# A decoder step in one core: prompt attention in pairs of heads, laid beside the sample attention

## The chip, the core and the metric

The kernel runs on one core of a Trainium2 chip. The engines are TensorE (PE, matrix products; PEld is its weight load), VectorE (DVE), ScalarE (ACT), GpSimd (POOL) and SyncE (SP), which here issues nearly all DMAs. SBUF is the working memory of 128 partitions, PSUM the memory of 8 banks into which PE writes. The metric is the device time of one execution in microseconds, as the median of several runs; one of them is profiled.

## The reference

Two layers of a hybrid decoder run on 256 prompt tokens and on 8 sample sequences of 8 new tokens each (320 tokens, width 2048, all in float32). The part that matters here is the attention of mixers A and C:

```
h = rms_norm(x, g_mix);  p = h @ w_in           # q, k, v of A and C, columns of B
A: 8 heads of 64, branches (window, dilation) = (128,1), (512,4), (2048,16)
C: 16 query heads, 2 kv heads, window 128, a learned sink per head
prompt: s = q k^T * scale; masked; p = exp(s - lse); o = p v     # 256 x 256 in blocks of 128
sample: the same with keys = concat(cache, new)                  # 8 sequences, 2048 (A) and 128 (C) old rows
x = x + concat(A, B, C) @ w_out;  x = x + SwiGLU(rms_norm(x))
```

Of the 2048 cached rows of A a sample needs 1280, the others lie outside every branch. Mixer B is a recurrence that is done before the attention begins.

## The kernel before

A layer streams the weights of `w_in` (each block is split into a high and a low part by ACT and DVE, and three products are summed), does mixer B, then the function `attention` of every engine, then `w_out` and the feed-forward blocks. All engines run programs of their own, in order, and wait for each other by named semaphores (`sc`, `sm`, `pn` and so on); the order is written out by hand.

The attention has two stages, one behind the other.

The prompt stage takes 24 heads (8 of A, 16 of C) in turn. GpSimd copies a head's queries into a zeroed tile `qp`, PE makes the scores (banks 0 and 1 in turn), DVE masks them into `psm` and takes two row maxima (`nm`), ACT takes exponentials with their sums, DVE scales by the reciprocals, PE turns the probabilities (three 128x128 transposes), ACT copies them to `ppt`, PE multiplies by the values and ACT copies the output into `pT`. Three heads are under way at once.

The sample stage takes four quarters q; a quarter is the pair of sequences 2q and 2q+1. The cached rows lie with positions on the partitions, and the scores need them with the head dimension there: in `keys`, PE transposes them in 26 turns of up to four 128x128 tiles, ACT copies each turn from PSUM into one of eight tiles `ktr`, and after every four turns PE makes the scores of that group, four products side by side on 128x32 column tiles of its array. The keys of quarter q+1 are turned ahead of the probabilities of quarter q. `probabilities` turns the sample's probabilities, `values` multiplies them by the cached values, `select` picks the wanted blocks; DVE's `scores`, `weighted` and `outputs` go with them. The caches are loaded by SP: `cK` and `cV` hold one quarter each, ten pieces of 512 KB for the keys of a quarter and ten for its values; the keys of the next quarter are loaded as the `ktp` count says that PE has turned a piece, its values as `pvq` says so.

SP stores the states of mixer B (18 DMAs from `Sout` and `SoutP`) and waits for them before it loads the first keys:

```
sp.wait_ge(sem["rw"], 2 * (l + 1))
sp.wait_ge(sem["souts"], 16 * 18 * (l + 1))
for which in "KV":
    for quad in range(3):
        cache(0, which, quad)
        cache(1, which, quad)
```

After the last quarter ACT and DVE split the first block of `w_out`, ACT writes the mixed rows `hh`, and PE begins the output projection.

## Time and profile before

| | |
|---|---|
| median of 3 runs | 3400.95 us (3396.55 to 3401.13) |
| the profiled execution | 3401.5 us, its span 3399.6 us |
| busy, share of the span | PE 96%, PEld 90%, DVE 50%, ACT 36%, POOL 3% |
| granted PE clock, mean | 0.979 of 2.4 GHz |
| DMA | 501.17 MB, mean 147 GB/s |
| attention, layer 0 | 468.6 to 660.4 us |
| attention, layer 1 | 2139.8 to 2334.1 us |

The busy shares are means over stages with different limits: most of the span is the weight stages, in which PE streams without a pause. The attention of a layer runs from PE's first scores of the prompt to its first product with `w_out`; it is read by itself, by stretches of the timeline.

### The profile page before, as it was taken

The page shows a single profiled execution, that of the slowest core. Times are in us where ns is not written, and L with a number is a line of the kernel's source. Part 1 is how long each engine was busy: PE and PEld are TensorE (multiplying, and loading weights), DVE is VectorE, ACT ScalarE, POOL GpSimd, SP SyncE. Part 2 cuts the span into 40 slices and gives each one's busy share as a digit, 9 for nine tenths or more (in the row PEclk, how much of TensorE's full clock was granted, in tenths as well). Part 3 has the DMA queues.
Part 4 walks back from the last instruction along what each step waited for, and adds up shares of the span by engine and source line. Part 5 has one row for each costly group of instructions (what it writes and reads, how often), then busy time and mean ns, then how long its engine had stood idle before and what let it go on. Part 6 is the DMA issues. An engine that isn't in the chain of part 4 may idle for free.

```text
span 3399.6 us, 60962 instructions
## 1 busy us (share of the span) xinstructions
PE 3272.0 (96%) x25078; PEld 3074.4 (90%) x25078; DVE 1711.3 (50%) x2269; ACT 1208.5 (36%) x1607; POOL 91.9 (3%) x209
## 2 busy tenths in 40 slices
PE   7999888999999999999999988889999999999998
PEld 6999755699999999999999986557999999999998
DVE  5455572355555454454545664714555544545544
ACT  3332256433322222222434313654422323323234
POOL 1000011000000000000000000100000000000000
PEclk9999889999999999999999998999999999999999
DMA  6552036765555554554564610577655545545454
GB/s 196 164 135 65 2 132 234 258 151 150 150 150 140 159 148 138 160 148 140 152 190 136 137 27 2 191 278 201 148 149 151 149 140 164 149 136 161 137 146 132
DMA packets 848704, 501.17 MB, mean 147 GB/s; under 512 B 96608, under 2 KB 823152, under 8 KB 848112
## 3 DMA queue, kind: packets, MB, share of 16 engines
q1 hardware_dynamic: 848108, 499.01, 51.7%
q8 instruction: 106, 1.74, 0.2%
q14 instruction: 38, 0.31, 0.0%
q10 hardware_dynamic: 452, 0.11, 0.0%
HBM read 485.71 MB, written 13.37 MB: 147 GB/s over the span
## 4 chain that ended last, share of the span: by engine, by line
PE 91%; DVE 4%; ACT 2%; issue 1%; DMA 1%; ACTq 0%; SPq 0%; DVEq 0%
PE PS L1435 87%; PE PS L1436 4%; ACT ktr L884 1%; ACT psm L855 0%; DVE psm L1303 0%; DVE wl L962 0%; ACT ppt L866 0%; DVE nm L1305 0%; ACT wh L641 0%; DVE S0T L1255 0%; DMA sink<-in_c_sink 0%; DVE rt L1080 0%; DMA raw<-in_w_out 0%; DVE WT L1183 0%; DMA raw<-in_w_in 0%
## 5 line engine op out<-in xcount | busy, mean ns | idle before, releaser
L641 ACT ACTIVATE wh<-raw 128x2048 fp32r<-128x2048 f32 (+1 forms) x408 | 711.7, 1744 | 1235.7 <-PE PS L1435 1214.2
L962 DVE TENSOR_TENSOR wl<-raw,wh 128x2048 fp32r<-128x2048 f32 (+1 forms) x408 | 848.9, 2081 | 400.2 <-ACT wh L641 399.6
L1435 PE MATMUL PS<-fh,wh 128*128 128x320 f32 x2816 | 870.6, 309 | 0.0
L1435 PE MATMUL PS<-fh,wl 128*128 128x320 f32 x2816 | 870.1, 309 | 0.0
L1435 PE MATMUL PS<-fl,wh 128*128 128x320 f32 x2816 | 870.1, 309 | 0.0
L1435 PEld LDWEIGHTS PS<-fh,wh 128*128 128x128 f32 x2816 | 528.5, 188 | 0.2
L1435 PEld LDWEIGHTS PS<-fl,wh 128*128 128x128 f32 x2816 | 528.5, 188 | 0.2
L1435 PEld LDWEIGHTS PS<-fh,wl 128*128 128x128 f32 x2816 | 528.5, 188 | 0.0
L1435 PE MATMUL PS<-hh,wh 128*128 128x320 f32 (+2 forms) x1696 | 521.3, 314 | 4.8 <-DVE wl L962 4.8
L1435 PE MATMUL PS<-hh,wl 128*128 128x320 f32 (+2 forms) x1696 | 513.5, 309 | 0.0
L1435 PE MATMUL PS<-hl,wh 128*128 128x320 f32 x1664 | 510.5, 310 | 0.0
L1435 PE MATMUL PS<-ah,wh 128*128 128x320 f32 x1408 | 435.7, 309 | 0.2 <-DVE wl L962 0.2
L1435 PE MATMUL PS<-al,wh 128*128 128x320 f32 x1408 | 435.1, 309 | 0.0
L1435 PE MATMUL PS<-ah,wl 128*128 128x320 f32 x1408 | 435.1, 309 | 0.0
L1435 PEld LDWEIGHTS PS<-hh,wh 128*128 128x128 f32 x1696 | 317.9, 191 | 8.6 <-DVE wl L962 5.2
L1435 PEld LDWEIGHTS PS<-hh,wl 128*128 128x128 f32 x1696 | 315.2, 189 | 0.0
L1435 PEld LDWEIGHTS PS<-hl,wh 128*128 128x128 f32 x1664 | 312.2, 188 | 1.4
L1435 PEld LDWEIGHTS PS<-ah,wh 128*128 128x128 f32 x1408 | 264.3, 188 | 0.8 <-issue 0.5
L1435 PEld LDWEIGHTS PS<-al,wh 128*128 128x128 f32 x1408 | 264.3, 188 | 0.0
L1435 PEld LDWEIGHTS PS<-ah,wl 128*128 128x128 f32 x1408 | 264.3, 188 | 0.0
L670 ACT ACTIVATE ge<-gt 128x320 f32<-128x320 f32 x88 | 41.5, 472 | 488.2 <-DVE gt L1002 488.2
L1002 DVE TENSOR_TENSOR gt<-PS,rsb 128x320 f32<-128x320 f32 x88 | 43.3, 492 | 224.7 <-PE PS L1435 224.6
(329 smaller groups left out, 2711.4 us busy)
## 6 DMA issues: line engine op xcount, KB each, us to landing
raw<-in_w_gate SPq DMA_DIRECT2D x88, 1024.0 KB, 5.6
raw<-in_w_up SPq DMA_DIRECT2D x88, 1024.0 KB, 5.6
raw<-in_w_down SPq DMA_DIRECT2D x128, 704.0 KB, 4.8
raw<-in_w_in SPq DMA_DIRECT2D x56, 1024.0 KB, 5.6
cK<-in_cache_a_k SPq DMA_DIRECT2D x80, 512.0 KB, 6.5
cV<-in_cache_a_v SPq DMA_DIRECT2D x60, 512.0 KB, 8.8
raw<-in_w_in SPq DMA_DIRECT2D x32, 512.0 KB, 5.3
raw<-in_w_out SPq DMA_DIRECT2D x32, 512.0 KB, 4.5
```

Source lines behind the costliest of these rows:

```text
L641: act.activation(wh[j][:, 0:kts], raw[j][:, 0:kts], ACT.Copy).then_inc(sem["wh"], 1)
L670: act.activation(ge[:], gt[:], ACT.Tanh, scale=0.5).then_inc(sem["gexp"], 1)
L884: act.activation(ktr[g % 8][:, 0:n], PS[:, 4 + g % 2, 0:n], ACT.Copy).then_inc(sem["ktc"], 1)
L962: tt(wl[j][:, 0:kts], raw[j][:, 0:kts], wh[j][:, 0:kts].bitcast(F32), ALU.subtract).then_inc(sem["wl"], 1)
L1002: tt(gt[:], PS[:, 0, 0:TOK], rsb[:], ALU.mult).then_inc(sem["ev"], 1)
L1435: mm = lambda out, lhsT, rhs, start=True, stop=True: pe.matmul(out, lhsT, rhs, start=start, stop=stop, skip_group_check=True)
L1436: tr = lambda out, x: pe.transpose(out, x, con[0:x.shape[0], at["ident"][0]:at["ident"][0] + x.shape[0]])
```

## The change

The prompt heads are taken in 12 pairs (4 of A, 8 of C), two heads in one instruction on DVE and two row halves of PE's array, with no copy of the queries. Pairs 0 to 2 start ahead; the other pairs lie in the quarters of the sample attention: in quarter q the carried pair 3q+2 is finished inside `keys`, pair a = 3q+3 goes between the scores and the probabilities, pair b = 3q+4 behind them, and pair c = 3q+5 is begun in `values` and carried over. ACT, not DVE, scales the probabilities.

The old keys are no longer turned by PE. DVE turns them where they lie, in 32x32 blocks (`turn`, six instructions a quarter, as the pieces land), and PE makes the scores on sixteen 32x32 tiles of its array: eight blocks of sixteen products over 320 columns each, every row group into a bank of its own (4 to 7). The queries for that are turned by `query_rows`, the window keys by `window_keys`. There is one tile `smA` and one `smC` instead of two. SP starts the first keys without waiting for the state stores, stores the states behind the keys of quarter 1, and loads the keys of quarter q+1 when all key scores of quarter q are done (`sc`). The diff, cut:

```diff
-        ktr = [place(f"ktr{i}", [P, 512], RW + 40960 + 2048 * i if i < 3 else RK + 2048 * (i - 3)) for i in range(8)]
+        kcT = place("kcT", [P, 2, P], RW + 40960)
+        qd = [place(f"qd{i}", [P, 2, 2, 2, 160], RK + 5120 * i) for i in range(2)]
...
                 def next_keys(q):
-                    for quad in range(3):
-                        sp.wait_ge(sem["ktp"], TURNS * (4 * l + q - 1) + (8 * (quad + 1) if quad < 2 else TURNS))
-                        cache(2 * q, "K", quad)
-                        cache(2 * q + 1, "K", quad)
+                    sp.wait_ge(sem["sc"], 4 * l + q)
+                    for b2 in range(2):
+                        for quad in range(3):
+                            cache(2 * q + b2, "K", quad)
...
+                for q in range(1, NB // 2):
+                    next_keys(q)
+                    if q == 1:
+                        states_out()
+                        sp.wait_ge(sem["souts"], 16 * 18 * (l + 1))
+                        for quad in range(3):
+                            cache(NB - 1, "V", quad)
+                    next_values(q)
...
+                def scale(p):
+                    i = p % 2
+                    take("prs")
+                    for h in range(2):
+                        for q, cols in enumerate(BLOCKS):
+                            a = act.activation(psm[i][:, h, cols], psm[i][:, h, cols], ACT.Copy, scale=sums[i][:, h, q:q + 1])
+                    a.then_inc(sem["pn"], 1)
...
+                for q in range(NB // 2):
+                    a, b, c = partners(q)
+                    carry = 3 * q + 2
+                    exp(carry)
+                    scale(carry)
+                    turned_probs(carry)
+                    if q < LASTQ:
+                        exp(a)
+                    output(carry)
+                    if q < LASTQ:
+                        scale(a)
+                        turned_probs(a)
+                        output(a)
+                    if q == 0:
+                        act.wait_ge(sem["snk"], 64 * (l + 1))
+                    exps(q)
+                    turned_sample(q)
+                    if q < LASTQ:
+                        query_rows(q + 1)
+                        exp(b)
+                        scale(b)
+                        turned_probs(b)
+                        output(b)
+                        window_keys()
...
+                def front(p):
+                    x = psm[p % 2]
+                    take("S")
+                    if p >= 2:
+                        dve.wait_ge(sem["PT"], 2 * (PAIRS * l + p - 1))
+                    m = C("maskA" if p < 4 else "maskC").unsqueeze(1).broadcast_to([P, 2, 384])
+                    done(stt(x[:], PS[:, 0:2, 0:384], SCALE, m, ALU.mult, ALU.add), "sm")
+                    dve.tensor_reduce(nm[p % 2][:, :, 0], x[:, :, 0:P], AX_X, ALU.max, negate=True)
+                    done(dve.tensor_reduce(nm[p % 2][:, :, 1], x[:, :, P:384], AX_X, ALU.max, negate=True), "nmx")
+                def back(p):
+                    i = p % 2
+                    take("pex")
+                    if p >= 4:
+                        done(tt(sums[i][:], sums[i][:], psk[i][:], ALU.add))
+                    done(dve.reciprocal(sums[i][:], sums[i][:]), "prs")
+                def turn(q, first, last):
+                    for n in range(first, last):
+                        b2, quad = n // 3, n % 3
+                        k0, kts = QUADS[quad]
+                        dve.wait_ge(*keys_in(l, q, quad, b2))
+                        x = cK[b2][:, k0:k0 + kts].rearrange("p k c -> p (k c)")
+                        dve.transpose(x, x).then_inc(sem["kt"], 1)
...
+                front(0)
+                turn(0, 0, 1)
+                back(0)
+                front(1)
+                turn(0, 1, 2)
+                back(1)
+                turn(0, 2, 4)
+                front(2)
+                turn(0, 4, 6)
                 for q in range(NB // 2):
+                    a, b, c = partners(q)
                     if q:
                         outputs(q - 1)
-                    if q < NB // 2 - 1:
-                        scores(q + 1)
+                    back(3 * q + 2)
+                    if q < LASTQ:
+                        front(a)
+                        back(a)
+                    scores(q)
+                    if q < LASTQ:
+                        front(b)
+                        turn(q + 1, 0, 5)
+                        back(b)
+                        turn(q + 1, 5, 6)
                     else:
                         split(start_of(l, "out"), 0, KT)
                     weighted(q)
-
-                dve.wait_ge(sem["oc"], 24 * (l + 1))
+                    if q < LASTQ:
+                        front(c)
...
+                def prompt_scores(p):
+                    if p:
+                        pe.wait_ge(sem["sm"], PAIRS * l + p)
+                    kt = KA + p if p < 4 else KC
+                    for cols, keys in ((slice(0, P), P), (slice(P, SEQ), SEQ)):
+                        for h in range(2):
+                            r = slice(h * HD, h * HD + HD)
+                            a = mm(PS[:, h, cols.start:cols.start + keys], pT[r, tile_of(p), cols], pT[r, kt, 0:keys])
+                    a.then_inc(sem["S"], 1)
+                def turned_probs(p, h):
+                    take("pn", 1 - h)
+                    if p or h:
+                        pe.wait_ge(sem["ptc"], 2 * (PAIRS * l + p) + h)
+                    for i in range(3):
+                        a = tr(PS[:, 2, i * P:(i + 1) * P], psm[p % 2][:, h, i * P:(i + 1) * P])
+                    a.then_inc(sem["PT"], 1)
+                def prompt_values(p):
+                    pe.wait_ge(sem["ptc"], 2 * (PAIRS * l + p) + 2)
+                    if p:
+                        pe.wait_ge(sem["oc"], PAIRS * l + p)
+                    if p >= 5 and p % 3 == 2:
+                        pe.wait_ge(sem["bo"], 4 * l + p // 3)
+                    for kt in range(2):
+                        for h in range(2):
+                            c0 = (2 * p + h) * HD if p < 4 else P + h * HD
+                            vals = tk[1 if p < 4 else 2][:, kt, c0:c0 + HD]
+                            out = PS[h * HD:h * HD + HD, 3, P * kt:SEQ]
+                            a = mm(out, vals, ppt[:, h, 0:SEQ] if kt == 0 else ppt[:, h, SEQ:384], kt == 0, kt == 1)
+                    a.then_inc(sem["O"], 1)
...
+                    a, b, c = partners(q)
+                    carry = 3 * q + 2
+                    pe.wait_ge(sem["ktc"], 8 * l + 2 * q + 2)
+                    pe.wait_ge(sem["kt"], 6 * (4 * l + q) + 6)
+                    if q:
+                        pe.wait_ge(sem["om"], 4 * l + q)
+                    for h in range(4):
+                        for jj in range(2):
+                            for i in range(4):
+                                r = slice(32 * i, 32 * i + 32)
+                                for b2 in range(2):
+                                    for fh in range(2):
+                                        out = PS[64 * b2 + 32 * fh:64 * b2 + 32 * fh + 32, 4 + i, 0:320].rearrange("p (k c) -> p k c", k=10)
+                                        c0 = (4 * fh + h) * HD + 32 * jj
+                                        m = mm(out, qd[q % 2][r, b2, jj, fh, 32 * h:32 * h + 32], cK[b2][r, :, c0:c0 + 32], not (h or jj), h == 3 and jj == 1)
+                            if (h, jj) == (3, 1):
+                                m.then_inc(sem["sc"], 1)
+                            if (h, jj) == (0, 0):
+                                if q:
+                                    select(q - 1)
+                                if q < LASTQ:
+                                    prompt_scores(a)
+                            elif (h, jj) == (1, 0):
+                                turned_probs(carry, 0)
+                            elif (h, jj) == (2, 0):
+                                turned_probs(carry, 1)
+                            elif (h, jj) == (3, 0):
+                                prompt_values(carry)
...
+                    keys(q)
+                    if q < LASTQ:
+                        for h in range(2):
+                            turned_probs(a, h)
+                        prompt_values(a)
+                        prompt_scores(b)
+                    probabilities(q)
                     values(q)
+                    if q < LASTQ:
+                        for h in range(2):
+                            turned_probs(b, h)
+                        prompt_values(b)
+                        window_keys(q + 1)
```

How the instructions stand before and after. On DVE, in the prompt stage before, where `psm_170` and `psm_171` are the tiles of two heads and a head's scaling stands behind the next one's maxima:

```order
L1303 SCALAR_TENSOR_TENSOR psm_170<-PS,con 128x384 [waits s_S,s_nmx]
L1304 TENSOR_REDUCE nm_179<-psm_170 128x1 [waits s_sm]
L1305 TENSOR_REDUCE nm_179<-psm_170 128x1
L1311 RECIPROCAL sums_181<-sums_181 128x2 [waits s_pex,s_nmx]
L1313 TENSOR_SCALAR psm_169<-psm_169,sums_181 128x128 [waits s_dve]
L1314 TENSOR_SCALAR psm_169<-psm_169,sums_181 128x256
```

And on DVE in quarter 0 after the change, from pair b's masking to the weighting of the quarter (`cK_139` and `cK_140` hold the keys of the next quarter's two sequences, `sums_167` the sums of pair b):

```order
L1336 SCALAR_TENSOR_TENSOR psm_160<-PS,con 128x768 [waits s_PT,s_S,s_bnm]
L1337 TENSOR_REDUCE nm_165<-psm_160 128x2 [waits s_sm]
L1338 TENSOR_REDUCE nm_165<-psm_160 128x2
L1354 STREAM_TRANSPOSE cK_139<-cK_139 128x2048 [waits s_cK00,s_nmx]
L1354 STREAM_TRANSPOSE cK_139<-cK_139 128x2048 [waits s_cK10]
L1354 STREAM_TRANSPOSE cK_139<-cK_139 128x1024 [waits s_cK20]
L1354 STREAM_TRANSPOSE cK_140<-cK_140 128x2048 [waits s_cK01]
L1354 STREAM_TRANSPOSE cK_140<-cK_140 128x2048 [waits s_cK11]
L1344 TENSOR_TENSOR sums_167<-sums_167,psk_169 128x4 [waits s_pex]
L1345 RECIPROCAL sums_167<-sums_167 128x4 [waits s_dve]
L1354 STREAM_TRANSPOSE cK_140<-cK_140 128x1024 [waits s_cK21,s_prs]
L1376 TENSOR_TENSOR ssu_173<-ssu_173,ssk_175 128x2 [waits s_bex]
```

The two scalings have left DVE, and five turns stand between a pair's maxima and its reciprocals, each behind a landing.

On PE, in the sample stage before, at a group of keys (`ktr_141` and the following are turned keys):

```order
L1436 MATMUL PS<-con,cK_140 128x128 [waits s_ktc]
L1436 MATMUL PS<-con,cK_140 128x128 x3
L1435 MATMUL PS<-ktr_141,qdA_151 32x512 [waits s_ktc]
L1435 MATMUL PS<-ktr_142,qdA_151 32x512
L1435 MATMUL PS<-ktr_143,qdA_151 32x512
```

And on PE after the change, inside the key scores of quarter 0, at the end of one block and the start of the next:

```order
L1492 MATMUL PS<-cK_139,qd_142 32x320 x2
L1492 MATMUL PS<-cK_140,qd_142 32x320 x2
L1493 MATMUL PS<-con,psm_160 128x128 [waits s_ptc,s_pn]
L1493 MATMUL PS<-con,psm_160 128x128 x2
L1492 MATMUL PS<-cK_139,qd_142 32x320 x2
```

The transposes of keys are gone, the scores read `cK` itself, and the carried pair's transposes, with their wait for ACT's scaling (`pn`), stand between the blocks.

On SP before, ahead of the first keys:

```order
L462 DMA out_new_wkv_sample<-Sout 64x4x64 [waits s_Sov,s_Soc]
L462 DMA out_new_wkv_sample<-Sout 64x4x64 x7
L464 DMA out_new_wkv_prompt<-SoutP 64x4x64
L462 DMA out_new_wkv_sample<-Sout 64x4x64 x8
L464 DMA out_new_wkv_prompt<-SoutP 64x4x64
L482 DMA cK_139<-in_cache_a_k 128x1x1024 [waits s_souts,s_rw]
```

And on SP after, from the last of quarter 1's keys to the first of its values:

```order
L480 DMA ckc_151<-in_cache_c_k 128x128
L508 DMA out_new_wkv_sample<-Sout 64x4x64 x8
L510 DMA out_new_wkv_prompt<-SoutP 64x4x64
L508 DMA out_new_wkv_sample<-Sout 64x4x64 x8
L510 DMA out_new_wkv_prompt<-SoutP 64x4x64
L476 DMA cX<-in_cache_a_v 128x1x1024 [waits s_souts]
L476 DMA cX<-in_cache_a_v 128x1x1024 x2
L478 DMA cX<-in_cache_a_v 128x1024 x2
L476 DMA cV_137<-in_cache_a_v 128x1x1024 [waits s_pvq]
```

The state stores have moved behind the keys of quarter 1, and the last sequence's values (`cX`), which wait for them, stand ahead of quarter 1's values and of quarter 2's keys.

## Rows read from the trace of the kernel before

**Rows 1.** Stretches of layer 0's two stages (busy us of each engine, clock, DMA share, GB/s).
```profile
468.60:528.80 60.20, 52.98 (x264) 32.13 (x264) 47.88 (x160) 45.84 (x161) 13.36 (x48) 0.97 0.74 268
528.80:660.40 131.60, 115.18 (x1060) 72.26 (x1061) 26.38 (x65) 72.07 (x162) 5.44 (x25) 0.96 0.72 252
...
sum 386.10, PE 337.29 PEld 209.31 DVE 148.62 ACT 235.80 POOL 37.22; mean PE 84.32 PEld 52.33 DVE 37.16 ACT 58.95 POOL 9.30
```

**Rows 2.** Timeline of PE at a score group (start us, us, what, idle before).
```profile
534.09 1.07 PE L1435 MATMUL PS<-ktr,qdA 128*32 128x512 f32 x8
535.08 1.09 PE L1436 MATMUL PS<-con,cK 128*128 128x128 f32 x8
```

**Rows 3.** Instructions on the tile psm (ns: least/median/most, first and last start).
```profile
L855 ACT ACTIVATE psm<-psm,nm x96: 401/447/495, 470.8 to 2197.7; 128x128 f32<-128x128 f32 x48, 128x256 f32<-128x256 f32 x48
L855 ACT ACTIVATION_READ_ACCUMULATOR psm<-psm,nm x96: 185/187/190, 471.1 to 2198.1; 128x1 f32 x96
L1303 DVE SCALAR_TENSOR_TENSOR psm<-PS,con x48: 557/558/558, 469.6 to 2196.0; 128x384 f32<-128x384 f32 x48
...
L1305 DVE TENSOR_REDUCE nm<-psm x48: 408/409/410, 470.3 to 2196.8; 128x1 f32<-128x256 f32 x48
```

**Rows 4.** Instructions on the tile ppt.
```profile
L866 ACT ACTIVATE ppt<-PS x48: 465/476/492, 474.9 to 2200.4; 128x384 f32<-128x384 f32 x48
```

**Rows 5.** DVE's groups by line and shape (busy us, mean ns, idle before).
```profile
L962 DVE TENSOR_TENSOR wl<-raw,wh 128x2048 fp32r<-128x2048 f32 x280 | 641.1, 2290 | 316.4 <-ACT wh L641 316.1
...
L1326 DVE SCALAR_TENSOR_TENSOR smA<-PS,con 128x512 f32<-128x512 f32 x16 | 10.3, 686 | 110.2 <-PE PS L1435 88.4 <-issue 21.7
...
L1057 DVE RECIPROCAL rsb<-rsb 128x320 f32<-128x320 f32 x4 | 8.6, 2154 | 2.4 <-ACT rsb L714 2.4
L1311 DVE RECIPROCAL sums<-sums 128x2 f32<-128x2 f32 x48 | 8.0, 166 | 1.7
...
L1117 DVE TENSOR_SCALAR pT<-pT 128x1280 f32<-128x1280 f32 x2 | 1.6, 820 | 0.0
```

**Rows 6.** Timeline of PE in mixer B, small tiles of the array.
```profile
309.55 0.69 PE L1435 MATMUL PS<-dA,dB 64*64 64x64 f32 x32
310.07 0.65 PE L1435 MATMUL PS<-dB,dA 64*64 64x64 f32 x32
...
452.34 1.24 PE L1435 MATMUL PS<-rstd,con 32*128 32x256 f32 x8
```

**Rows 7.** Timeline of DVE, ACT and PE in the sample stage.
```profile
549.66 1.62 DVE L1326 SCALAR_TENSOR_TENSOR smA<-PS,con 128x512 f32<-128x512 f32 x3 [23.57 <-PE PS L1435]
...
553.44 0.54 DVE L1332 TENSOR_REDUCE snm<-smC 128x2 f32<-128x384 f32 x1
...
641.14 1.42 ACT L891 ACTIVATE smA<-smA,snm 128x1344 f32<-128x1344 f32 x1 [1.51 <-DVE snm L1332]
...
643.43 0.28 ACT L895 ACTIVATE ssk<-snm,snk 128x2 f32<-128x2 f32 x1
...
645.99 1.42 PE L1436 MATMUL PS<-con,smA 128*128 128x128 f32 x11
...
648.77 0.64 PE L1435 MATMUL PS<-tk,ptA 64*32 64x256 f32 x8
...
658.72 1.06 PE L1435 MATMUL PS<-con,om 128*128 128x32 f32 x4 [3.44 <-DVE omC L1344]
```

**Rows 8.** Stretches around a pause of PE (columns as in rows 1).
```profile
553.00:556.10 3.10, 0.19 (x3) 0.04 (x1) 0.99 (x2) 2.08 (x4) 0.00 (x0) 0.82 0.01 3
556.10:560.00 3.90, 3.90 (x17) 1.91 (x18) 0.00 (x0) 2.64 (x8) 0.00 (x0) 0.50 0.15 23
```

**Rows 9.** SP's first key loads, and how long the key loads took to land.
```profile
L482 SPq DMA_DIRECT2D cK<-in_cache_a_k x6: 535/603/622, 482.7 to 486.6; - x6
...
DMA to landing us min/median/max: 4.0/7.7/10.3
```

**Rows 10.** A stretch of key loads in the sample stage.
```profile
592.00:596.00 4.00, 3.75 (x29) 2.37 (x30) 0.00 (x0) 2.58 (x5) 0.00 (x0) 1.00 1.01 401
```

425 lines of the change are left out of this document (169 added, 256 removed).

## The prediction, made before the changed kernel ran

> **What bounds the kernel now.** I read the windows first. The page gives TensorE (PE) 96% of the span, but that share is made by the weight stages; the change touches two stages only, one per layer. In layer 0 the prompt attention takes 60.2 us and the sample attention 131.6, up to the first product of the output projection; with layer 1 the four stretches add up to 386.1 us [rows 1], 193 a layer. Nothing is full there: over the sample stretch VectorE (DVE) works 26.4 of 131.6 us, ScalarE (ACT) 72.1, DMA 0.72 of its time. So each stage is a chain, and time comes out of it only by shortening the chain or laying two side by side. In the prompt stretch DVE (47.9 of 60.2) sets the pace: per head a 0.56 us masking, two maxima (0.41 the wider), two scalings [rows 3]. In the sample stretch PE and ACT alternate: four transposes, one copy to SBUF, 26 times a quarter; then a score group, whose successor starts 0.99 us later [rows 2].
>
> **The change, part by part.** Time 0 is PE's start of attention (468.6 us in layer 0); the end is the first output-projection product. Before: 191.8 and 194.3 us.
>
> *Removed:* 104 transposed key tiles a layer and their ACT copies, GpSimd's query copies (hidden already), the 60 us of prompt heads as a stage of their own. *Added:* DVE turns, 10,240 columns a quarter; 128 small score products a quarter.
>
> *A turn.* No row shows one. From below it is bounded by the fastest DVE form, 820 ns for 1280 columns (0.64 per column); from above by the dearest, 2154 for 320 (6.7) [rows 5]. I take 1.07 ns, since the forms that move a 4-byte column per beat lie there: 686 ns for 512, 2290 for 2048. So 2.2 us for 2048 columns, 1.1 for 1024, 11 a quarter. The Trainium skill (Vector Engine (DVE) Microarchitecture Reference, the reshape front-end section) lets the transpose sustain one element per cycle per lane; no run here shows it yet, and by it the sum stays.
>
> *A score block* (16 products of 32x32, 320 columns). Sixteen-fold tiling has no row. Four column tiles do run together: 512 columns take 0.99 us for the whole group [rows 2], which scales to 0.62 for 320. Four row tiles do too, and 64x64 tiles, two by two: 32 records start within 0.52 us [rows 6], which also shows 32 records can issue in that time. I take 0.6; the bounds are 0.5 (issue alone) and 2.5 (row groups one after another). The Trainium skill (TensorEngine Tiling (Array Packing), Key Properties) says that changing the tiling mode drains the engine, which speaks against mixing these blocks with full-array work. In the rows the full-array transposes start 0.99 us after a column-tiled group whose records last 1.07 [rows 2], so a drain is not visible; at 0.15 us, 14 switches a round would add 2 us a round, 16 in all.
>
> *A prompt pair.* DVE: one masking of 768 columns (0.56 for 384 plus 1.0 ns a column: 0.94), maxima over 256 and 512 columns, 0.41 and 0.67: 2.0 us [rows 3, 5]. ACT: exponentials 2 x 1.0 (two of 0.45 with 0.19 readings between), two sinks of 0.28 [rows 7]; DVE's reciprocal and sum 0.17 each [rows 5]; ACT scaling, four copies of 0.27 to 0.38 by the 0.48 for 384 columns [rows 4]: 1.3; two turns by PE (0.5) and copies (0.48); value products 0.85.
>
> *A round* (quarter q in the middle), from PE's start of the key scores, with the carried pair masked by then: exponentials to 2.5, reciprocals 2.9, scaled 4.2; PE turns head 0 to 4.8, two blocks, head 1 to 6.5, two blocks to 7.7, values 8.5, last block **9.1**. Only there is `sc` given, and the next keys may load. The new-token and window scores end at 10.9. DVE's masks and maxima, 4.3 us for three pieces [rows 7] and 0.4 for the fourth, end at 15.7 (the next pair fits in before). ACT's exponentials take 2.6 (641.14 to 643.71), PE's turns and ACT's copies 2.8 (645.99 to 648.77) [rows 7]: 21.1. The value products took 6.5 (648.77 to 658.72, less the 3.44 of idle); with the query rows and a pair's scores 28.5. DVE meanwhile: pair b to 17.7, five turns (9.8) to 27.5, back(b) 27.9, the last turn 29.1, weighting 30.5, next pair 32.5. The keys are there in time: issued at 9.1, first landing after 4.0 us [rows 9], 5.4 MB at 401 GB/s [rows 10] take 13.4. Pair b ends the round, as its reciprocal stands behind five turns: 27.9, scaling 29.2, two turns and copies 31.6, values 32.6, window keys copied **33.6**.
>
> *The other rounds.* In round 0 the carried pair already has its exponentials, so `sc` comes at 6.8 and the round is 2.3 shorter: 31.3. In round 1 SyncE (SP) issues the state stores (18 at some 0.6 us [rows 9]), waits for their landing, then cX and V, before it reaches the keys of quarter 2; those then land some 6 us late, of which 3.2 show: 36.8. Round 2: 33.6. *Front:* DVE masks the first pair, waits for the first two key pieces (issue, 4.0 us to landing, one piece more: 5.5), then does six turns (11), two pairs (4.0), two reciprocals (0.4) and waits about 1.7 for the second pair's exponentials: 22.6. *End:* round 3 to 21.1, then as before 11.65 (648.77 to 660.40). Sum 22.6 + 31.3 + 36.8 + 33.6 + 32.7 = 157.0.
>
> *The clock.* Between pair b's scores (14.4) and the turned probabilities (18.3) PE idles 3.9 us a round. Where it idled 3 us before, the next 3.9 ran at a granted 0.50, the 1.2 GHz level [rows 8]. That stretches the probabilities and the first values by about 2.4 us: four times, **166.6**. Against 193.05 that is 26.4 a layer, 52.9 in all.
>
> The profiled execution took 3401.5 us (span 3399.6), the median is 3400.95, so 3401.5 - 52.9 = 3348.6; I say **3348 us**. A change under 0.2% (7 us) can't be told from none.
>
> *What stands behind the new waits.* DVE's turns wait for landings, with the pair's reciprocals and the weighting of the quarter behind them, and PE's next key scores behind those. SP's key loads wait for `sc`, with the state stores and the V loads behind. PE's turning of a pair waits for ACT's scaling, with the rest of the key blocks behind it; ACT's query rows and pair b wait behind the sample's exponentials.
>
> *Edits costed at nothing:* the query rows on PE and ACT lie under the value products and DVE's turns; the moved state stores leave the front free (14 us of SP there) and cost what round 1 says; GpSimd's memsets end before time 0.
>
> **Rivals.**
> - *The DVE becomes the bound (slower).* The place is the five turns in front of back(b). At twice my price rounds 0 to 2 grow by 9.8 each (9216 columns), the front by 11 (10,240): some 40 a layer, about 3430. It decides from the point where these 37,900 columns eat the 26.4 us that a layer gains: 0.7 ns more, 1.8 a column. For it: no row shows a turn, and 2154 ns for 320 columns is a DVE row too. Against: every form that only moves or adds lies at 1.1 or below.
> - *The blocks run row group by row group (slower):* 2.5 us instead of 0.6; then the blocks, not the carried pair, set `sc`: 22.5 for 9.1. Four times 13.4: about 3455. Against: [rows 6]. The Trainium skill (TensorE: Matmul & The Clock Gate, Measured speedup vs the span model) gives 10.6-fold for sixteen tiles; an estimate from that is 0.94 a block, which would make the sum about 3370.
> - *The clock stays low through the stage.* Some 10 us more a round, as blocks, values and turns double: about 3428. For it: one 3 us pause gives half the clock [rows 8], and a round has a pause of 3.9 us, one of 1.4 in front of the carried pair's turn, and about 1 us around each copy that PE waits for. Against: the window of [rows 10], in an alternation of quarter-microsecond waits, stayed at 1.00.
> - *The gap goes unpunished and the steps pack tighter:* 157 a layer and a quicker turn at 0.64: 3305 to 3330.
> - *The change doesn't do what it says:* PE takes its instructions in order, so each wait for a pair stands in front of the samples too; at 45.5 us a round, (191.8 - 22.6 - 32.7)/3, nothing is saved: within 0.2%.
>
> **How the numbers follow.** Forecast (3325 to 3375) 0.54, tighter 0.20, no gain 0.06, DVE bound 0.09, blocks in series 0.04, low clock 0.07. The tighter case reaches to about 3300 and holds most of its chance above that; of the dear ones the low clock and the small excesses are taken in: 3300 to 3410 leaves out about 2 in 10. Faster 0.78 (forecast, tighter, and half of the low clock's chance, where it holds for a part of the rounds), same 0.05, slower 0.17.
>
> **What the profile after would show.** Right: STREAM_TRANSPOSE at 2.2 us for 2048 columns; a block's 16 products within 0.6 us; rounds of 33 to 38 us, whose ends are chained PE - ACT - DVE through pair b; key loads starting some 9 us into a round; stretches at 0.5 clock around the probabilities; nothing moved in the weight stages. Wrong if turns cost over 1.8 ns a column, if `sc` comes after 15 us, if the DVE waits for landings (then SP's order is the bound), or if a round ends in the value products instead of pair b.

## The result, and the profile after

The changed kernel takes 3379.4 us (median of 5 runs, 3377.8 to 3385.9) against 3396.6 us for the kernel before on the same chip: a ratio of 0.995, 95% interval 0.9935 to 0.9964. It is faster, by 17 us, and the time lies within the range; but the forecast was a gain of 52.9 us, three times as much. The profiled execution has a span of 3380.0 us, 19.6 less than before. The attention of layer 0 now takes 180.8 us (before 191.8 [rows 1], forecast 166.6), that of layer 1 182.4 (before 194.3). Between the two layers' attentions the profile shows 1483.2 us for 1479.4 before; in the later runs this stretch took 1477 to 1485 without a pattern, and I draw nothing from it.

The page's first part, whose PE share answers to the 96% of before:

```profile
PE 3198.1 (95%) x26358; PEld 3021.7 (89%) x26358; DVE 1757.8 (52%) x2117; ACT 1150.6 (34%) x1543; POOL 74.3 (2%) x157
```

The windows of layer 0's attention, cut where the key scores of a round begin (front, rounds 0 to 2, last stretch; columns as in [rows 1]):

```profile
467.52:490.91 23.39, 10.70 (x61) 5.83 (x56) 17.54 (x18) 13.42 (x48) 0.00 (x0) 0.58 0.98 367
490.91:528.20 37.29, 29.61 (x483) 17.36 (x484) 23.42 (x33) 18.46 (x62) 1.93 (x12) 0.90 0.80 275
528.20:575.24 47.04, 33.43 (x492) 19.72 (x492) 24.56 (x39) 20.92 (x74) 1.93 (x12) 0.80 0.97 377
575.24:614.02 38.78, 31.76 (x491) 19.40 (x492) 24.20 (x39) 20.90 (x74) 0.00 (x0) 0.84 0.46 170
614.02:648.31 34.29, 24.19 (x413) 14.72 (x414) 8.79 (x21) 15.56 (x35) 1.93 (x1) 0.80 0.60 148
```

Two things stand out. Round 1 is 8 to 10 us longer than its neighbours, and DMA is full in it (0.97, 377 GB/s). And the granted clock, 0.97 and 0.96 in the two stages before [rows 1], is 0.58 to 0.90 now, although TensorE is busy for 29 to 33 us of each of rounds 0 to 2.

The turns, among the groups by line and shape in layer 0:

```profile
L1354 DVE STREAM_TRANSPOSE cK<-cK 128x2048 f32<-128x2048 f32 x16 | 36.5, 2296 | 11.5 <-DMA cK<-in_cache_a_k 11.3
...
L1354 DVE STREAM_TRANSPOSE cK<-cK 128x1024 f32<-128x1024 f32 x8 | 9.8, 1224 | 0.1
```

The timeline of the changed kernel, the places that the rest speaks of:

```profile
490.91 1.38 PE L1492 MATMUL PS<-cK,qd 32*32 32x320 f32 x32 [2.21 <-DVE cK L1354]
...
511.49 10.12 DVE L1354 STREAM_TRANSPOSE cK<-cK 128x2048 f32<-128x2048 f32 x5
...
512.14 2.57 PE L1493 MATMUL PS<-con,smA 128*128 128x128 f32 x11 [3.38 <-ACT ssk L900]
...
521.91 1.49 ACT L879 ACTIVATE psm<-psm,sums 128x128 f32<-128x128 f32 x4 [1.99 <-DVE sums L1345]
...
524.17 0.55 PE L1493 MATMUL PS<-con,psm 128*128 128x128 f32 x3
...
529.17 1.89 SPq L476 DMA_DIRECT2D cX<-in_cache_a_v  x3
...
540.33 2.83 SPq L476 DMA_DIRECT2D cK<-in_cache_a_k  x3
...
556.12 2.31 DVE L1354 STREAM_TRANSPOSE cK<-cK 128x2048 f32<-128x2048 f32 x1 [7.52 <-DMA cK<-in_cache_a_k]
...
569.57 0.90 PE L1493 MATMUL PS<-con,psm 128*128 128x128 f32 x3 [5.47 <-ACT psm L879]
...
580.03 2.80 PE L1492 MATMUL PS<-cK,qd 32*32 32x320 f32 x64
...
619.01 1.71 PE L1492 MATMUL PS<-cK,qd 32*32 32x320 f32 x64
...
642.47 2.29 DVE L994 TENSOR_TENSOR wl<-raw,wh 128x2048 fp32r<-128x2048 f32 x1 [11.66 <-ACT wh L634]
...
646.34 0.48 DVE L1380 SCALAR_TENSOR_TENSOR om<-PS,ssu,con 128x256 f32<-128x256 f32 x1 [1.30 <-PE PS L1492]
```

Read from the top. The first key block of round 0 (16 products, two records each) takes 1.38 us, at half clock. In round 0 the five turns (four of 2048 columns and one of 1024) run through without a wait (10.1 us, forecast 9.8). The pause ahead of the probabilities is 3.4 us (forecast 3.9), and the 11 transposes behind it take 2.6 us, where they took 1.42 before [rows 7]. At 524.17 TensorE turns pair b without having waited, since ScalarE finished scaling it 0.8 us before: pair b does not end this round, but it is close. In round 1 the keys of quarter 2 are issued from 540.33 and their first turn starts at 556.12, after a wait; that ends in 5.47 us for which TensorE waits for pair b. Two key blocks (64 records) take 2.80 us at half and 1.71 at full clock. The last two rows are the split of `w_out` and, behind it on VectorE, the weighting of the last quarter, which waits another 1.30 us for TensorE's values; both become important below.

### The profile page after: what moved, and what is told of

It is laid out like the page before. It is cut to its first block and busy times, and to the rows that moved or that the text cites. A ratio compares the mean times of both kernels' runs of the same rounds, so it can differ in the third digit from the quotient of the medians.

```text
span 3380.0 us, 62858 instructions
## 1 busy us (share of the span) xinstructions
PE 3198.1 (95%) x26358; PEld 3021.7 (89%) x26358; DVE 1757.8 (52%) x2117; ACT 1150.6 (34%) x1543; POOL 74.3 (2%) x157
```

## The experiments

**Theory**, from these rows: (a) the transfers of round 1 are late because cX (2.6 MB) and the values of quarter 1 are being carried ahead of the keys of quarter 2; (b) TensorE loses time at half clock, in more places than the pause that the prediction priced. **Rivals**: pair b's chain behind five turns (the forecast), products that stand in each other's way on one row group, or a round that is simply full on TensorE.

All ratios are to the kernel before, timed beside each run on the same chip; the changed kernel itself stands at 0.995.

| run | ratio, 95% interval | median us |
|---|---|---|
| e1_cx_late | 0.9917 (0.9902 to 0.9933) | 3372.7 |
| e2_fill | 0.9947 (0.9933 to 0.9960) | 3381.6 |
| e3_back_early | 0.9942 (0.9928 to 0.9956) | 3379.5 |
| e4_row_order | 0.9946 (0.9932 to 0.9960) | 3379.4 |
| e5_fill_sized | 0.9953 (0.9940 to 0.9966) | 3381.2 |
| e6_late_fill_back | 0.9873 (0.9859 to 0.9887) | 3355.0 |
| e7_fill_all | 0.9854 (0.9841 to 0.9868) | 3349.0 |
| e8_half_rows | a single run | 3402.6 |
| e9_late_back | 0.9908 (0.9893 to 0.9924) | 3366.0 |
| e10_out_first | 0.9842 (0.9829 to 0.9856) | 3344.5 |
| e11_fill_no_late | 0.9905 (0.9889 to 0.9920) | 3363.5 |
| e12_half_columns | 1.0164 (1.0147 to 1.0181) | 3454.9 |
| e13_light_fill | 0.9913 (0.9893 to 0.9932) | 3366.3 |

### e1_cx_late: cX behind the keys of quarter 2

```diff
                     if q == 1:
                         states_out()
+                    if q == 2:
                         sp.wait_ge(sem["souts"], 16 * 18 * (l + 1))
                         for quad in range(3):
                             cache(NB - 1, "V", quad)
```

> Only SyncE's order is changed: the values of the last sequence (2.6 MB into cX, needed by the last quarter alone) are loaded behind the keys of quarter 2 and not ahead of the values of quarter 1. Theory, the transfers of round 1 (cX, the values of quarter 1 and the keys of quarter 2, 13.4 MB at some 400 GB/s) are what makes it 47.0 us: the keys of quarter 2 land some 6 us earlier, pair b's wait of 5.5 us and the half clock behind it go, round 1 of layer 0 comes down to 39 to 41 us, round 2, which then starts at full clock, from 38.8 to about 37; 8 to 11 us a layer, 16 to 22 in all: 3358 to 3364 us. Rival, the round is long because of its own chain through TensorE and the DMAs only show it: under 4 us in all.

Its timeline in round 1 of layer 0:

```profile
552.52 10.02 DVE L1355 STREAM_TRANSPOSE cK<-cK 128x2048 f32<-128x2048 f32 x5
...
564.37 0.55 PE L1494 MATMUL PS<-con,psm 128*128 128x128 f32 x3 [0.53 <-ACT psm L880]
```

The five turns no longer wait, pair b's wait falls from 5.47 to 0.53 us, and round 1 comes to 41.1 us in both layers (47.0 and 48.7 before). So the wait was the transfers'. But the kernel gains 6.7 us by the medians (11 by the ratios of the table), where 16 to 22 were expected: round 2 did not fall (39.8 and 40.7), and round 0 of layer 1 took 41.0 instead of 37.2, both at half clock for part of the time.

### e2_fill, e5_fill_sized: filling the pause ahead of the probabilities

```diff
                         prompt_scores(b)
+                    fill(20 if q < LASTQ else 48)   # 12 and 27 in the second run
                     probabilities(q)
+                def fill(n):
+                    for _ in range(n):
+                        mm(PS[:, 2, 0:P], C("ident"), C("ident"))
```

> TensorE multiplies 20 (last quarter 48) 128x128 products of the identity into the free bank 2 in the pause ahead of the sample's probabilities; nothing reads them. Theory, each such pause costs by the half clock behind it alone: the probabilities take 1.4 us everywhere instead of up to 2.6, the values no longer 12 but 10.7 us, 2 to 2.5 us a round, 16 to 20 us in all. Rival, in rounds 0 and 2 pair b's chain on VectorE and ScalarE (five turns, reciprocal, scaling) comes only 0.5 to 0.8 us behind today's values, in round 1 the keys end last: 0.5 to 0.8 us in rounds 0 and 2, nothing in round 1, 2 in the last: 6 to 8 us in all. A third: the clock does not follow such products, no change.

```profile
509.10 4.73 PE L1492 MATMUL PS<-con 128*128 128x128 f32 x40
513.67 1.36 PE L1493 MATMUL PS<-con,smA 128*128 128x128 f32 x11
...
528.32 1.38 PE L1492 MATMUL PS<-cK,qd 32*32 32x320 f32 x32 [0.47 <-ACT kcT L857]
```

The clock does follow: the transposes behind the products take 1.36 us instead of 2.57. But 20 products last 4.7 us, more than the pause, and the next round begins at half clock all the same (1.38 us for its first block). The second run has the number corrected.

> As the first filling, but 12 products in the pause ahead of the probabilities (27 in the last quarter), since one took 0.23 us and 20 of them overran the pause of 3.4 us by 1.3. Theory, half clock behind the pauses is a cost of the changed kernel: with the pause filled and not overrun, rounds 0 and 2 are 0.8 to 1.5 us shorter, the last stretch 34.3 to about 31: 4 to 6 us a layer, 8 to 12 in all: 3367 to 3372 us. Rival, what is won is lost again at the next pause (the clock falls there instead): within 3 us of the changed kernel.

No gain either (3381 us): the rival holds, as far as these pauses go. But what is won is not lost to the clock alone. In rounds 0 and 2 TensorE now waits for pair b's scaling, which was ready before it in the changed kernel:

```profile
523.20 0.55 PE L1493 MATMUL PS<-con,psm 128*128 128x128 f32 x3 [1.24 <-ACT psm L879]
...
607.89 0.55 PE L1493 MATMUL PS<-con,psm 128*128 128x128 f32 x3 [0.53 <-ACT psm L879]
```

So with the pauses filled the forecast's chain, five turns and then the reciprocal, does end these rounds. The last stretch is the telling one. Its rows, of TensorE, ScalarE and VectorE in the order of time:

```profile
624.05 6.25 PE L1492 MATMUL PS<-con 128*128 128x128 f32 x54
631.36 1.42 PE L1493 MATMUL PS<-con,smA 128*128 128x128 f32 x11 [1.06 <-ACT ssk L900]
...
639.02 1.91 ACT L634 ACTIVATE wh<-raw 128x2048 fp32r<-128x2048 f32 x1 [4.93 <-DMA raw<-in_w_out]
641.04 2.29 DVE L994 TENSOR_TENSOR wl<-raw,wh 128x2048 fp32r<-128x2048 f32 x1 [12.34 <-ACT wh L634]
...
643.65 0.48 DVE L1380 SCALAR_TENSOR_TENSOR om<-PS,ssu,con 128x256 f32<-128x256 f32 x1
...
644.70 1.06 PE L1492 MATMUL PS<-con,om 128*128 128x32 f32 x4 [4.04 <-DVE omC L1382]
```

TensorE ran the values at full clock and was done at 640.7, and the stretch still took 34.5 us (34.3 in the changed kernel). VectorE weights the quarter only after the split of the first `w_out` block, ScalarE starts that split at 639.02, and it waits for the block's landing. In the changed kernel the weighting began 1.30 us behind the split, when the values came; so the half clock stood 1.3 us above the load there, and with the half clock gone the load alone keeps the stretch as long.

### e3_back_early: pair b's reciprocal behind four turns

```diff
-                        turn(q + 1, 0, 5)
+                        turn(q + 1, 0, 4)
                         back(b)
-                        turn(q + 1, 5, 6)
+                        turn(q + 1, 4, 6)
```

> Pair b's reciprocal stands behind four turns instead of five on VectorE. As the prediction had it (pair b ends each round, behind five turns) this takes 2.0 us off rounds 0 to 2: 12 us in all. Rival, by the trace of the changed kernel: TensorE reaches pair b's transposes without waiting in rounds 0 and 2 of layer 0 (0.5 us of wait in round 0 of layer 1) and waits for late keys in round 1: 0 to 4 us in all.

No change, 3379.5 us. The forecast's own statement of what ends a round falls with it, for the changed kernel: pair b is ready 0.8 and 0.6 us before TensorE comes to it in rounds 0 and 2 of layer 0, so by itself the reciprocal's place is worth nothing. It counts once TensorE comes sooner, as in the filled kernel above.

### e4_row_order: the row groups in turn

```diff
-                            for i in range(4):
-                                r = slice(32 * i, 32 * i + 32)
-                                for b2 in range(2):
-                                    for fh in range(2):
+                            for b2 in range(2):
+                                for fh in range(2):
+                                    for i in range(4):
+                                        r = slice(32 * i, 32 * i + 32)
```

> In each block of key scores the four row groups now alternate from one product to the next, instead of four products in a row on one row group; the same products otherwise. Theory, products on one row group follow each other and that is why a block takes 0.84 us and not the 0.6 of the prediction: a block comes to 0.55 to 0.65, 1.5 to 2.3 us a round, 12 to 18 us in all. Rival, the block is bound by something that the order does not touch: 0.80 to 0.87 a block and no change (within 4 us).

Two blocks still take 1.71 us at full clock, and the kernel 3379.4 us. The order of the products is not what sets a block.

### e6_late_fill_back, e9_late_back: the edits together

The edits of e1, e3 and e5 in one kernel.

> Three edits together: cX behind the keys of quarter 2, 12 and 27 products in the pauses, pair b's reciprocal behind four turns. If the transfers and the clock are separate costs, they add: 7 to 10 us from the first, 8 to 12 from the second, and the third now counts, since TensorE comes to pair b earlier: 1 to 3: 3355 to 3364 us. Rival, the cost of the clock moves to the next pause: 3368 to 3373, as with the first edit alone.

3355.0 us, at the fast edge of what was expected: 24.4 us less than the changed kernel, where the three alone brought 6.7, nothing and nothing. To see what the filling did in it, it was taken out again:

> The third run of the last four without its filling: cX behind the keys of quarter 2 and pair b's reciprocal behind four turns, no products in the pauses. It tells what the filling was worth there. Theory, the half clock: without the filling 10 to 16 us of the 24 go, 3365 to 3372 us, and TensorE is at half clock for 60 us or more of a layer's attention. Rival, the reciprocal's place was what pays once the keys come in time, and the filling does little, as it did alone: 3352 to 3360 us.

3366.0 us, within what the theory named. So cX and the reciprocal bring 13 us, the filling another 11. (The profiled execution of this kernel is the longest of its runs, 3380.6 us, 14 us above the next; rounds 0 to 2 take 41 us each there, at a granted clock of 0.76 to 0.83, so these rows may overstate the half clock.)

### e7_fill_all, e11_fill_no_late: all pauses filled

```diff
+                fill(10)              # behind the first two pairs' scores
                 for h in range(2):
                     turned_probs(0, h)
...
                 def turned_probs(p, h):
+                    if h and p and p % 3 != 2:
+                        pe.wait_ge(sem["oc"], PAIRS * l + p)
+                        fill(2, 3)        # pairs a and b, into bank 3
                     take("pn", 1 - h)
...
                 def prompt_values(p):
-                    pe.wait_ge(sem["ptc"], 2 * (PAIRS * l + p) + 2)
                     if p:
                         pe.wait_ge(sem["oc"], PAIRS * l + p)
+                    if p and p % 3 != 2:
+                        fill(2, 3)
+                    pe.wait_ge(sem["ptc"], 2 * (PAIRS * l + p) + 2)
...
                 def keys(q):
...
+                    fill(1 if q else 6)
...
                 def values(q):
+                    fill(3)
...
+                fill(4)
                 select(NB // 2 - 1)
```

with cX late, the reciprocal early and 12 (27) products ahead of the probabilities as above.

> As the run before, and the smaller pauses of TensorE are filled too: two products of 0.23 us in each pause of 0.6 to 0.7 us between a pair's transposes and its values, three ahead of the sample values, one ahead of the key scores, four ahead of the last selection, ten in the first pair's pause and six ahead of the first key scores. Theory, the half clock is brought on by TensorE's pauses all together, the half-microsecond ones too: the stage runs at 0.95 or more, the first key block of a round takes 0.83 us instead of 1.38, rounds come to 34 to 35.5, the last stretch to 31: 3335 to 3350 us. Rival, only the pauses of 3 us and more count: as the run before, within 4 us. A third, the products collide with what they wait for and the rounds grow.

3349.0 us, within the theory's numbers; the rounds of layer 0 take 34.7, 37.5 and 35.9 us at 0.95, 0.95 and 1.00, and only the last stretch stays, at 35.8. That is 6.0 us less than without the filling of the small pauses, though the two intervals still overlap a little. The profiles agree: over both layers the fronts, where longer pauses were filled as well, are 1.3 us shorter, and rounds and last stretches together 6.0. So the half-microsecond pauses seem to count, by some 6 us. Then the late cX was taken back, with all pauses filled:

> All pauses filled and pair b's reciprocal behind four turns, but cX again ahead of the values of quarter 1. Theory, the transfers of round 1 and the clock are two costs: round 1 stays at 44 to 47 us and the other rounds at 34.5 to 37, so 16 to 20 us over the kernel with both: 3365 to 3369 us. Rival, the late keys cost mainly by the half clock that their wait brings: 3352 to 3360 us.

3363.5 us, below the theory's range and nearer to it than to the rival's. Round 1 is 47.1 us again, at a clock of 0.89:

```profile
527.17:574.27 47.10, 34.60 (x539) 23.81 (x539) 24.42 (x39) 20.52 (x73) 1.93 (x12) 0.89 0.93 356
574.27:608.48 34.21, 32.34 (x542) 22.18 (x543) 24.22 (x40) 20.75 (x74) 0.00 (x0) 1.00 0.60 225
```

With the reciprocal early in all four, the kernel takes 3379.5 with neither, 3366.0 with cX late, 3363.5 with the pauses filled, 3349.0 with both: 13.5 and 16.0 us one by one, 30.5 together. By the ratios of the table it is 11.5 and 12.6 one by one and 30 together, each with some 7 us of uncertainty either way. They are two costs, and within that they add.

### e10_out_first: the first blocks of w_out ahead of the last values

```diff
                 for q in range(1, NB // 2):
                     next_keys(q)
...
+                    if q == LASTQ:
+                        sp.wait_ge(sem["out"], 16 * 9 * (l + 1))
+                        sp.wait_ge(sem["pvq"], 12 * l + 9)
+                        stream(l, "out", part="first")
                     next_values(q)
-                sp.wait_ge(sem["out"], 16 * 9 * (l + 1))
-                sp.wait_ge(sem["pvq"], 12 * l + 9)
-                stream(l, "out")
+                stream(l, "out", part="rest")
```

> As the kernel with all pauses filled, and SyncE loads the first two blocks of w_out ahead of the last quarter's values (their place is free once the values of quarter 2 are multiplied), not behind. Theory, the last stretch is bound by that load: its block lands at 639 us, ScalarE and VectorE split it, and the weighting of the last quarter stands behind the split on VectorE (TensorE pauses 4.0 us there with all other pauses filled, and the stretch stayed at 34.3 to 34.5 us when it ran at full clock). The stretch falls from 35.6 to 31 to 33 us: 5 to 9 us in all, 3340 to 3344 us. Rival, the prompt rows (four ScalarE copies of some 1 us each) and the values end the stretch: within 2 us of 3349.

3344.5 us, the best version, 0.9842 of the kernel before. Its windows in layer 0:

```profile
466.41:489.25 22.84, 15.24 (x100) 11.20 (x95) 17.59 (x18) 13.45 (x49) 0.00 (x0) 0.78 0.98 367
489.25:523.79 34.54, 31.89 (x532) 21.28 (x532) 23.15 (x32) 18.07 (x62) 1.93 (x12) 1.00 0.86 301
523.79:559.19 35.40, 33.11 (x539) 22.29 (x539) 23.00 (x37) 20.51 (x73) 1.93 (x12) 1.00 1.00 377
559.19:595.19 36.00, 32.95 (x539) 22.24 (x539) 25.44 (x42) 20.68 (x73) 0.00 (x0) 1.00 0.87 327
595.19:626.51 31.32, 28.73 (x481) 20.60 (x482) 9.11 (x22) 15.29 (x36) 1.93 (x1) 1.00 0.55 140
```

and the rows that answer to those of the last stretch above:

```profile
617.71 1.92 ACT L640 ACTIVATE wh<-raw 128x2048 fp32r<-128x2048 f32 x1
...
619.73 2.29 DVE L1000 TENSOR_TENSOR wl<-raw,wh 128x2048 fp32r<-128x2048 f32 x1 [7.29 <-ACT wh L640]
...
624.54 0.48 DVE L1386 SCALAR_TENSOR_TENSOR om<-PS,ssu,con 128x256 f32<-128x256 f32 x1 [2.24 <-PE PS L1498]
```

ScalarE splits without waiting, and the weighting now waits for TensorE's values, not the other way round. The stretch falls to 31.3 us (33.0 in layer 1). The gain by the medians, 4.5 us, is just below the 5 to 9 expected, and the two intervals overlap; the rows, not the medians, show the cause: the two last stretches are 7.0 us shorter together.

### e8_half_rows, e12_half_columns: what a block costs

```diff
-                            for i in range(4):
+                            for i in range(2):
```

> Only row groups 0 and 1 of the key scores are computed, eight products a block instead of sixteen (half of the old keys' scores are left out). Theory, the products of a block are issued one after another at a fixed price, 52 ns each at full clock: the block falls from 0.83 to about 0.42 us, sc comes 3.3 us earlier. Rival, the row groups run side by side and the 320 columns set the time: 0.7 to 0.83 us, sc hardly earlier.

```profile
492.00:506.00 14.00, 13.72 (x150) 5.17 (x150) 2.34 (x6) 4.90 (x17) 0.00 (x0) 0.50 0.72 278
```

```profile
495.12 2.38 PE L1492 MATMUL PS<-cK,qd 32*32 32x320 f32 x32
```

Half the products, and the kernel takes 3402.6 us in a single run, 23 more than with all of them. Two blocks take 2.38 us, against 2.80 for full blocks at the same half clock. So a block of eight products is not half as dear: something other than their number bounds it there. I take that to be the passing of its columns, which the run does not show. And the clock stood at 0.50 for 14 us in which TensorE was busy for 13.72: work was removed and time was lost (mean granted clock 0.946, in the changed kernel 0.962). The run leaves the price at full clock open, so the products were made smaller instead, on the best version:

```diff
-                                        m = mm(out, qd[q % 2][r, b2, jj, fh, 32 * h:32 * h + 32], cK[b2][r, :, c0:c0 + 32], not (h or jj), h == 3 and jj == 1)
+                                        for ks in (slice(0, 5), slice(5, 10)):
+                                            m = mm(out[:, ks], qd[q % 2][r, b2, jj, fh, 32 * h:32 * h + 32], cK[b2][r, ks, c0:c0 + 32], not (h or jj), h == 3 and jj == 1)
```

> On the kernel with all pauses filled and the first blocks of w_out loaded early: each product of the key scores is made as two of 160 columns (32 products a block instead of 16, the same result). It tells what the 0.84 us of a block at full clock are. Theory, a fixed price for each product (its weight load and its issue, 52 ns): the block doubles to some 1.67 us, sc comes 6.7 us later in each of the four rounds and the kernel is up to 53 us slower (3375 to 3400 us). Rival, the columns that pass set the time (320 columns take 0.62 us by the column tiles of the kernel before, the rest is filling and draining): 0.84 to 1.1 us a block, within 10 us of 3344.

```profile
493.34 1.66 PE L1498 MATMUL PS<-cK,qd 32*32 32x160 f32 x64 [2.50 <-DVE cK L1360]
...
499.59 1.72 PE L1498 MATMUL PS<-cK,qd 32*32 32x160 f32 x37 [1.46 <-issue]
...
502.07 5.62 PE L1498 MATMUL PS<-cK,qd 32*32 32x160 f32 x128
```

```profile
486.00:499.40 13.40, 9.27 (x199) 7.40 (x200) 9.15 (x10) 4.96 (x16) 0.00 (x0) 1.00 1.04 409
499.60:517.50 17.90, 17.90 (x371) 12.99 (x370) 0.18 (x1) 4.49 (x15) 0.00 (x0) 0.50 0.18 63
```

The block doubles at full clock: 64 records in 1.66 us, 26 ns each, as in a block of 320 columns (32 records in 0.83). A product of this kind has a fixed price of 52 ns, for 160 columns and for 320; what makes it is not shown. By that alone the kernel would lose 53 us; it loses 110. The rest goes with the clock. It stood at 1.00 up to 499.4 us, the end of a pause of 1.46 us inside the blocks (the profile shows nothing that TensorE waited for), and from 499.6 on at 0.50 for 17.9 us in which TensorE does not pause at all. Whether the pause or the small products brought the clock down is not shown; that 17.9 us of unbroken work on them did not bring it back is.

### e13_light_fill: the same pauses, filled with little

That left a question: is it the pauses that bring on the half clock, or what the array does? The filling products of the best version were made on one 32x32 tile instead of 128x128.

```diff
-                        mm(PS[:, bank, 256:384], C("ident"), C("ident"))
+                        mm(PS[0:32, bank, 256:384], C("ident")[0:32, 0:32], C("ident")[0:32])
```

> The kernel with all pauses filled and the first blocks of w_out loaded early, but each filling product is made on one 32x32 tile of the array instead of all 128x128 (the same 128 columns, so about the same 0.2 us). Theory, the clock follows TensorE's pauses: with the pauses filled by anything it stays as it was with full products, 10 to 15 us at half clock in a layer's attention, 3344 us within 4. Rival, the clock follows what the array does: half clock comes back as without filling, 50 us or more a layer, rounds of 36 to 41 us, 3360 to 3368 us.

3366.3 us (3357 to 3376): 22 us of the gain are gone, though TensorE is as busy as with full products. Its front and its last stretch in layer 0, and round 0 of layer 1:

```profile
467.68:491.30 23.62, 16.67 (x102) 10.59 (x96) 17.59 (x18) 13.45 (x49) 0.00 (x0) 0.69 0.98 362
...
601.50:636.10 34.60, 33.37 (x482) 23.09 (x482) 8.79 (x21) 15.42 (x35) 1.95 (x1) 0.85 0.50 128
...
2139.80:2180.93 41.13, 39.66 (x535) 23.40 (x533) 23.44 (x33) 18.41 (x63) 1.94 (x12) 0.80 0.79 272
```

In the last stretch TensorE is busy for 33.4 of 34.6 us and is granted 0.85; with full products it had 1.00 at 28.7 of 31.3 us. The rival holds in the time. In the clock it holds in part: rounds 0 to 2 of layer 0 stand at 0.92 to 0.95, but round 0 of layer 1 takes 41.1 us at 0.80. As 2 x (1 - clock) x length, the half clock comes to 38 us in layer 0 and 52 in layer 1; in the best version it is 10 and 7. How much of the half clock a pause makes and how much an emptier array stays open.

## Why the prediction was wrong

Two steps of the sum failed, the one that makes round 1 late and the one that prices the clock at one pause; one term, the key block, was too small, and pair b does not end the rounds. By the prediction's own steps, the forecast with its clock term spread over rounds and end, and what was measured in layer 0:

| us | forecast | changed kernel | best version |
|---|---|---|---|
| front | 22.6 | 23.4 | 22.8 |
| round 0 | 33.7 | 37.3 | 34.5 |
| round 1 | 39.2 | 47.0 | 35.4 |
| round 2 | 36.0 | 38.8 | 36.0 |
| last stretch | 35.1 | 34.3 | 31.3 |
| sum | 166.6 | 180.8 | 160.1 |

**Right.** A turn: 2.30 us for 2048 columns and 1.22 for 1024, forecast 2.2 and 1.1; the five turns of a round, 9216 columns, took 10.1 us, forecast 9.8. The price was better than its reason: of the rows behind it, 686 ns for 512 columns are 1.34 a column and 2290 for 2048 are 1.12 [rows 5], not "1.1 or below". The Trainium skill's rule (Vector Engine (DVE) Microarchitecture Reference, the reshape front-end section), one element per cycle per lane, agrees as far as the step from 1024 to 2048 columns shows it: 1.05 ns a column, where those two rows differ by 1.04. VectorE bounds no round; in the front TensorE waits 2.21 us for its last turn, as forecast. The front: 23.4 for 22.6. The pause ahead of the probabilities: 3.4 for 3.9. From the probabilities to the end of round 0: 16.1, forecast 15.3 and 2.4 for the clock. The blocks do run row group beside row group, and a full-array transpose between two blocks shows no drain that the rows could tell (for the 0.15 us of the prediction there is no row).

**Wrong: round 1.** The step was "those then land some 6 us late, of which 3.2 show". The direction was right and the mechanism not. I had counted SyncE's issues; but SyncE reached the keys of quarter 2 when `sc` came (540.15 and 540.33), not later. What was late was the landing: in the 11 us before, cX and the values of quarter 1 had been issued, 7.9 MB, which at the 377 GB/s of this round take 21 us, and the keys went behind them. The prediction's own sign for this, VectorE waiting for landings, is in the rows: 11.3 us in layer 0, 7.52 of them ahead of the first turn of this round. With cX moved the round falls by 6 us in layer 0 and 7.6 in layer 1, and the kernel by 13.5 us where pair b's reciprocal is early in both.

**Wrong: the clock.** The step was "that stretches the probabilities and the first values by about 2.4 us: four times". The stretch behind the pause was about right; that it was the only place was not. Key blocks, the front and whole runs of values stand at half clock: from the windows, as 2 x (1 - clock) x length, some 72 of the 180.8 us of layer 0's attention, against 14 of 191.8 before [rows 1]. The rival of a low clock had the mechanism (a mean of 0.80 to 0.90 in the rounds, not 0.5) but was given 0.07. Filling the pauses with full products is worth 16 to 17 us in the whole kernel, with cX early or late (13 and 18 by the ratios). I had read [rows 8] as a price per pause. The change also takes 104 full-array transposes a layer away and puts products on 32x32 tiles in their place; that such products can leave the clock low is shown by the run with half columns, where it stood at 0.50 with TensorE busy throughout. The changed kernel's own blocks, of 320 columns, ran at 1.00 in three rounds of the best version, so there the filled pauses were enough. The trace of the kernel before had the sign, in mixer B, mostly on 64x64 tiles and behind a pause of 3 us:

```profile
440.00:452.00 12.00, 12.00 (x34) 3.27 (x33) 5.21 (x7) 1.67 (x5) 0.00 (x0) 0.50 0.03 7
```

Twelve microseconds without a pause stayed at half clock there, where [rows 8] shows only 3.9.

**Mis-sized: the block.** 0.84 us, not 0.6. The bound "issue alone", 0.5, was taken from 64x64 tiles that started 32 records in 0.52 us [rows 6]; on 32x32 tiles a record takes 26 ns. The Trainium skill (TensorE: Matmul & The Clock Gate, the section "Wait — 56ns, not 53.3ns?") gives a floor of some 25 ns between two starts however few the columns are; an estimate from that is 0.80 us for 32 records, which these blocks agree with and the 64x64 tiles, with a start every 16 ns, do not. So why a record takes 26 ns here stays open. Eight blocks a round make 1.9 us of it, some 15 us in the two layers, of which a part lay under other waits. With the clock it makes `sc` late: 10.4 to 13.9 us into the rounds of layer 0, where 6.8 (round 0) and 9.1 were forecast. The 6.8 was also too low for another reason: eight blocks, a pair's scores, two turns and its values are more than 7 us of TensorE's own work even at my prices, and at half clock in part.

**Wrong: what ends a round.** Not pair b behind five turns, though by little. In layer 0 TensorE's own work ends rounds 0 and 2, 0.8 and 0.6 us behind pair b's scaling, and the keys end round 1. With the pauses ahead of the probabilities filled and five turns still in front, pair b does end rounds 0 and 2, by 1.24 and 0.53 us. With the keys in round 1 and the load in the last stretch, that leaves this filling alone little to win.

**Right, with a bound unseen: the last stretch.** 34.3 us for 35.1. The forecast came from the chain through the values and half a clock, and in the changed kernel the weighting does wait last for the values. But only 1.30 us ahead of that stands the landing of the first `w_out` block, whose split VectorE makes before the weighting of the last quarter; with the clock held it sets the stretch. The row of the 3.44 us that TensorE waits for `omC` was in my table [rows 7]; I took it out of the rounds' values and left it in the 11.65 us of the end without asking what it waited for. It was the same split:

```profile
655.05 2.29 DVE L962 TENSOR_TENSOR wl<-raw,wh 128x2048 fp32r<-128x2048 f32 x1 [5.72 <-ACT wh L641]
```

The sum: of the 36 us that were missing, cX and the filled pauses give back 30.5 and the early `w_out` 4.5. That the best version comes to 3344.5 us, near the forecast, is no proof of the forecast: it has neither the clock term nor the late keys in it, and still needs 160.1 us in layer 0 for the 157.0 of the sum at full clock; the blocks alone are 7.7 us of a layer over their price.

## What to carry to other kernels

Price a load by the bytes that are on their way ahead of it, not by when its queue issues it; and put what is needed last behind what is needed next. When full-array work is replaced by small tiles, look at the granted clock of the stretch as a cost of its own, and count the products: on 32x32 tiles each had a fixed price here, 52 ns. An edit that brings nothing alone may bring its due once another bound is gone: try them together, and take one out again, before calling any of them useless.

## What the runs showed of the hardware

- TensorE can stand at half clock while it is busy without a pause: 0.50 over 17.9 us, 17.9 of them busy, with 160-column products on 32x32 tiles; 0.50 over 12.0 us, all busy, mostly on 64x64 tiles in the kernel before; 0.50 over 14.0 us, 13.7 busy, with eight tiles at work. The Trainium skill (TensorE: Matmul & The Clock Gate, the section on HAM oscillation) names waits as the cause. A pause stands ahead of each of these stretches too (1.46, 3.02 and 3.84 us); that the clock then stays low through unbroken work is what the runs add.
- Less work can take longer: leaving out half of the key products added 23 us in a single run, with a mean granted clock of 0.946 for 0.962.
- Products that nobody reads, on the whole array, in pauses as short as 0.6 us, held the clock at 1.00 through three rounds of 34.5 to 36.0 us; the same pauses filled on one tile did not bring the time.
- A product on a 32x32 tile costs 52 ns at full clock (two records of 26 ns) with 160 columns as with 320, and some 88 ns at half clock (128 records of 160 columns in 5.6 us).
